# A two-block transformer kernel: the low parts of 18 weight blocks move from VectorE (three: from nowhere) to GpSimd

## The reference, cut to what matters

```
h = rms_norm(x, g_pre) * (1 + scale) + shift          # scale, shift, gate from w_ada
proj = h @ w_in                                        # 2048 x 20032
a  = mla_branch(...) * silu(z_mla);  y_mla = a @ w_mla_proj
bb = dilated_branch(...) * silu(z_dil);  y_dil = bb @ w_dil_proj
x  = x + gate * rms_norm((sigmoid(g1) * y_mla + sigmoid(g2) * y_dil) @ w_o, g_post)
h2 = x @ w_in_a  ->  sparse attention with indexer, gate  ->  @ w_out_a
x  = layer_norm(ALPHA * x + y);  x = x + (p @ w_ple) * sigmoid(x @ w_ple_gate)
x @ w_kv_b, x @ w_q_b  ->  stick-breaking attention, gate  ->  @ w_out_b  ->  norm, gate
```

## Time and profile before

| | |
|---|---|
| median of 3 runs | 2376.17 us (2375.61 to 2376.22) |
| the profiled execution | 2375.65 us, span of its records 2374.3 us |
| TensorE clock granted | full over the whole span |
| TensorE, VectorE, ScalarE, GpSimd busy | 99%, 62%, 48%, 4% |
| split blocks | 781; mean VectorE low part 1.185 us, mean ScalarE high part 1.025 us |
| HBM | 201 GB/s over the span, about 400 in the first 120 us |

### The profile page before, as it was taken

The page is one execution under the profiler, slowest core; times in us unless marked ns, Lnnn a source line. Parts: engine busy times, 40 slices in busy tenths (PEclk is TensorE's granted clock), DMA queues, the critical chain, the costliest instruction groups (busy, mean ns, idle before and its releaser), DMA issues.

```text
span 2374.3 us, 28762 instructions
## 1 busy us (share of the span) xinstructions
PE 2351.3 (99%) x11224; PEld 1965.6 (83%) x11224; DVE 1464.9 (62%) x1997; ACT 1140.7 (48%) x1471; POOL 87.2 (4%) x121
## 2 busy tenths in 40 slices
PE   9999999999999999999999999999999999999999
PEld 5688898988889988888888888888788788888777
DVE  7887765554555455686756675566765555456675
ACT  4344454544445554443444445554545555455453
POOL 0000100000000000000000100000200000000020
PEclk9999999999999999999999999999999999999999
DMA  9986643555554457887655555455665555555565
GB/s 397 401 298 207 196 148 115 173 178 188 188 165 146 139 186 253 288 291 241 213 195 191 181 174 162 163 165 185 223 213 188 169 177 167 185 161 177 187 221 177
DMA packets 131241, 478.98 MB, mean 202 GB/s; under 512 B 15281, under 2 KB 15537, under 8 KB 125985
## 3 DMA queue, kind: packets, MB, share of 16 engines
q1 hardware_dynamic: 126080, 458.41, 58.4%
q0 software_dynamic: 3728, 17.76, 2.1%
q10 hardware_dynamic: 1298, 0.97, 0.1%
HBM read 470.80 MB, written 6.29 MB: 201 GB/s over the span
## 4 chain that ended last, share of the span: by engine, by line
PE 90%; DVE 5%; ACT 2%; DMA 2%; issue 1%; SPq 0%; POOL 0%; ACTq 0%; DVEq 0%; POOLq 0%
PE G L841 25%; PE G L843 25%; PE G L842 25%; PE A L852 4%; DMA ada<-in_weights 2%; DVE wlo L1472 2%; PE A L841 2%; PE A L843 2%; PE A L842 2%; PE A L923 1%; PE A L903 1%; PE G L837 1%; ACT whi L1128 1%; PE A L996 1%; DVE CP L1780 1%
## 5 line engine op out<-in xcount | busy, mean ns | idle before, releaser
L1472 DVE TENSOR_TENSOR wlo<-raw,whi 128x1024 fp32r<-128x1024 f32 (+3 forms) x781 | 922.9, 1185 | 698.2 <-ACT whi L1128 695.9
L1128 ACT ACTIVATE whi<-raw 128x1024 fp32r<-128x1024 f32 (+3 forms) x781 | 800.0, 1025 | 832.3 <-PE G L843 744.5
L841 PE MATMUL G<-whi,XH 128*128 128x512 f32 (+3 forms) x2804 | 1082.1, 386 | 9.1 <-DVE wlo L1472 6.8
L843 PE MATMUL G<-whi,XL 128*128 128x512 f32 (+3 forms) x2804 | 1066.7, 380 | 0.0
L842 PE MATMUL G<-wlo,XH 128*128 128x512 f32 (+3 forms) x2804 | 1065.7, 380 | 0.0
L841 PEld LDWEIGHTS G<-whi,XH 128*128 128x128 f32 x2804 | 526.7, 188 | 105.2 <-DVE wlo L1472 12.7
L843 PEld LDWEIGHTS G<-whi,XL 128*128 128x128 f32 x2804 | 526.3, 188 | 95.1
L842 PEld LDWEIGHTS G<-wlo,XH 128*128 128x128 f32 x2804 | 526.9, 188 | 90.2 <-issue 0.2
L841 PE MATMUL A<-whi,XH 128*128 128x512 f32 x192 | 77.2, 402 | 3.0 <-DVE wlo L1472 3.0
L1486 DVE CUSTOM_DVE_ANT_0 ada<-ada,dil 128x2048 f32<-128x2048 f32 x32 | 75.1, 2347 | 5.0 <-DMA ada<-in_weights 4.9
L842 PE MATMUL A<-wlo,XH 128*128 128x512 f32 x192 | 74.7, 389 | 0.0
(11 more groups left out here) (230 smaller groups left out, 1551.1 us busy)
## 6 DMA issues: line engine op xcount, KB each, us to landing
raw<-in_weights SPq DMA_DIRECT2D x724, 512.0 KB, 3.6
ada<-in_weights SPq DMA_DIRECT2D x32, 1024.0 KB, 11.2
raw<-in_weights SPq DMA_DIRECT2D x80, 384.0 KB, 3.1
raw<-in_weights SPq DMA_DIRECT2D x16, 288.0 KB, 2.9
spill<-nat POOLq DMA_DIRECT2D x8, 512.0 KB, 5.4
CP<-spill POOLq DMA_DIRECT2D x8, 512.0 KB, 6.5
raw<-in_weights SPq DMA_DIRECT2D x8, 336.0 KB, 3.2
FT<-in_xT SPq DMA_DIRECT2D x4, 512.0 KB, 5.7
```

Of the source, the lines that this page charges most:

```text
L841: pe.matmul(acc, xh[:, k, half], wh, start=(k == start), stop=False)
L843: ins = pe.matmul(acc, xl[:, k, half], wh, start=False, stop=(k == end - 1))
L1128: ac.activation(whi[r % NSPL][:, 0:2 * cols], raw[o.home[n]][:, 0:2 * cols], ACT.Copy).then_inc(hi_done, 1)
L1472: ve.tensor_tensor(wlo[r % NSPL][:, 0:2 * cols], raw[o.home[n]][:, 0:2 * cols], whi[r % NSPL][:, 0:2 * cols].bitcast(F32), ALU.subtract).t ...
```

## The change

Slots 18, 21 and 27 leave the set of unsplit slots, so they get a high part and a low part like all others. The low parts of 18 slots (`GP_LOW`), among them these three, are made by GpSimd with the same subtraction, at the take's place in GpSimd's walk. They count on a semaphore of their own, `lo_gp`; `o.low[s]` is the count up to slot s on whichever of the two semaphores slot s uses. TensorE and the loads wait on that one.

```diff
-WHOLE = frozenset([*range(OPENING), 6, 9, 12, 15, 18, 21, 27])
+WHOLE = frozenset([*range(OPENING), 6, 9, 12, 15])
+
+GP_LOW = frozenset([18, 21, 27, 33, 39, 45, 52, 58, 94, 469, 541, 643, 646, 675, 678, 707, 710, 743])
...
+        self.low = {s: sum(x not in self.whole and (x in GP_LOW) == (s in GP_LOW) for x in range(s + 1))
+                    for s in range(len(self.slots))}
@@ TensorE, in slot(s) @@
-                pe.wait_ge(lo_done, o.rank[s] + 1)
+                pe.wait_ge(lo_gp if s in GP_LOW else lo_done, o.low[s])
@@ VectorE, in take(n) @@
+                if o.slot_of[n] in GP_LOW:
+                    return
@@ GpSimd @@
+        def take(n):
+            kind, w, c0, cols, k = plan[n]
+            if kind == "w" and o.slot_of[n] in GP_LOW:
+                r = o.rank[o.slot_of[n]]
+                gp.wait_ge(hi_done, r + 1)
+                gp.tensor_tensor(wlo[r % NSPL][:, 0:2 * cols], raw[o.home[n]][:, 0:2 * cols],
+                                 whi[r % NSPL][:, 0:2 * cols].bitcast(F32), ALU.subtract).then_inc(lo_gp, 1)
...
-                gp.wait_ge(lo_done, o.rank[65] + 1)
+                gp.wait_ge(lo_done, max(o.low[s] for s in range(66) if s not in o.whole and s not in GP_LOW))
...
         for kind, a, b in o.walk:
-            if kind == "move":
+            if kind == "take":
+                take(a)
+            elif kind == "move":
                 move(a)
@@ SyncE, in load(n) @@
-                    sp.wait_ge(lo_done, o.rank[s] + 1)
+                    sp.wait_ge(lo_gp if s in GP_LOW else lo_done, o.low[s])
```

More of the change, by code:

```diff
@@ L642, in first_and_second_block @@
     moved = [sem(f"moved_G{n}") for n in range(4)] + [sem(f"moved_A{n}") for n in range(4)]
-    hi_done, lo_done, modulated, gated = (sem(n) for n in ("hi_done", "lo_done", "modulated", "gated"))
+    hi_done, lo_done, lo_gp, modulated, gated = (sem(n) for n in ("hi_done", "lo_done", "lo_gp", "modulated", "gated"))
     x_hi, x_lo, side_hi, rows_made, rows_gp = (sem(n) for n in ("x_hi", "x_lo", "side_hi", "rows_made", "rows_gp"))
```

## The result

| | before | after |
|---|---|---|
| median | 2376.19 us (2375.61 to 2376.82, 4 runs) | 2387.03 us (2386.08 to 2388.22, 4 runs) |
| the profiled execution | 2375.65 us | 2388.22 us |
| ratio, 95% interval | | 1.0041 (1.0029 to 1.0054) |

The account below looks back on a forecast made before the run. TensorE's matmul issue rate was taken to bound the kernel, except where VectorE hands over a low part late. Terms 0.3 - 1.65 + 0.9 - 1.4 + 1.0 + 6.6 - 0.4 = +5.35 gave 2381.5 us, range 2378 to 2386.

Parts of the forecast that it names:

- opening, to slot 35: Slots 18, 21, 27: 2.2 us of TensorE time saved, lost at slot 33 behind VectorE's product until 120.34; +0.3.
- slot 52: TensorE's idle 1.42 us goes, as GpSimd makes the low part by 172.95; -1.65, between -1.7 and 0.
- slot 94: VectorE's rotation steps and the two adds that empty slot 94's banks slide; +0.9.
- slot 469: VectorE issues first, GpSimd works 1357.6 to 1359.9, and the wait goes; -1.4, or +0.9 if GpSimd is first.
- slot 541: VectorE's later steps and the XL that slot 541 multiplies slide to 1594.0; +1.0.
- three pairs, clock full: Slots 643/646, 675/678, 707/710: two holds per pair delay VectorE's low part between them; +2.2 a pair, +6.6 together.
- slot 743: Idle 0.22 us, one VectorE step behind it, the exponential after that just in time; -0.4, if not +0.6.
- h: Time one 1024-column GpSimd low part keeps VectorE from its own work: 2.15 us, bounds 0 and 2.6.
- A wait costs its idle time and about 0.3: Price of each TensorE wait: its idle time plus about 0.3 us, as the pipe refills.
- Rival 2: No change: the hold does not reach the scans and VectorE's wide product; +0.2, 2376.4 us; chance 0.17.
- Rival 1: Faster: h near 0, every term a gain, 10.1 us with the opening held to 1; 2366 us; chance 0.23.
- rival 3: Slower still: GpSimd first at 469 (+0.9), slots 21 and 33 stall the opening (+1.5); 2385 us; chance 0.07.

Follow-up runs that it names:

- three_gp: The kernel before with only the low parts of slots 52, 469 and 743 on GpSimd; 2372.83 us, ratio 0.9984.
- after_fill4: The changed kernel with four extra 384-column TensorE products, results unused, ahead of slots 645, 677 and 709; 2382.70 us, ratio 1.0024.
- pairs_gp: The kernel before with only the low parts of slots 643, 646, 675, 678, 707 and 710 on GpSimd; 2385.33 us, ratio 1.0036.
- open_dve: The kernel before with slots 18, 21 and 27 split and every low part on VectorE; 2376.74 us, ratio 0.9998.
- open_late: open_dve with ScalarE's wait for a small load moved from slot 22 to slot 42, the loads still issued at 22; 2375.17 us, ratio 0.9995.
- tt_beside: The kernel before plus a 1024-column GpSimd scratch subtraction, which nothing waits for, at the six takes of the pairs; 2386.06 us in one run.
- memset_beside: tt_beside with two GpSimd memsets of scratch tiles in place of each subtraction; 2376.44 us in one run.
- ordered: The kernel before with low parts 52 and 469 on GpSimd and ten VectorE steps issued later, behind the low part due next; 2369.57 us, ratio 0.9967.
- open_gp: The changed kernel with only the low parts of slots 18, 21 and 27 on GpSimd, the other fifteen on VectorE; 2377.58 us, ratio 1.0002.
- best: ordered with slots 18, 21, 27 split on VectorE and ScalarE's small-load step, loads included, moved from slot 22 to 42; 2371.17 us, ratio 0.9976.

## Why the prediction was right in direction and short in size

Each term of the sum, in us longer (+), beside the steps of the table:

| | forecast | after | where else it shows |
|---|---|---|---|
| opening, to slot 35 | +0.3 | +2.7 | +0.1 to +1.8 in kernels whose opening is unchanged |
| slot 52 | -1.65 | -1.67 | three_gp -1.66 |
| slot 94 | +0.9 | +0.87 | after_fill4 +0.87 |
| slot 469 | -1.4 | -1.4 | three_gp -1.37 |
| slot 541 | +1.0 | +1.15 | after_fill4 +1.15 |
| three pairs, clock full | +6.6 | +6.1 | 2.1 each in pairs_gp, after_fill4 |
| clock at half behind two of them | none | +3.4 | gone in after_fill4 |
| slot 743 | -0.4 | -0.2 | three_gp -0.2 |
| clock at half behind slot 745 | none | +1.5 | three_gp, open_dve have it, open_late not |

- **h, the time one GpSimd low part keeps VectorE away: right.** 2.15 was forecast from 128- and 512-column rows. The step of 0.68 takes 2.88 (2.20 more), two scans 3.42 for 1.27 (2.15 more), the wide product up to 4.49 for 2.34 (2.15 more). In the second and third pair the second hold falls on the step behind the scans (L1788, 2.68 for 0.69), at the same price. GpSimd alone takes 2.40 at its shortest, as forecast. That both operands must lie in SBUF shows at slot 45: beside GpSimd's low part VectorE adds a product in PSUM to a tile in SBUF in its usual 0.69 (GpSimd, then VectorE):

```profile
153.66 2.40 POOL L2064 TENSOR_TENSOR wlo<-raw,whi 128x1024 fp32r<-128x1024 f32 x1 [13.34 <-ACT whi L1132]
```
```profile
153.89 0.69 DVE L1556 TENSOR_TENSOR kept<-A,kept 128x512 f32<-128x512 f32 x1 [0.48 <-PE A L847]
```

- **Rival 2 (the hold does not reach scans and the wide product): out.** Both rows just named. tt_beside shows the scans held by work that nothing waits for.
- **Rival 1 (h near 0): out**, by the same rows and by tt_beside against memset_beside. Its gains exist where VectorE has nothing due: three_gp.
- **Slots 52, 94, 469, 541: right to 0.2 us.** At 541 TensorE waits 1.66 us for XL, at 94 1.09 for VectorE's adds, as the prediction named them. At 469 VectorE was first by 0.04 us (1358.39 against 1358.43), so that half of rival 3 did not come true, by little; its other half, a stalled opening, did.

```profile
276.98 0.47 PE L845 MATMUL G<-whi,XH 128*128 128x512 f32 x1 [1.09 <-DVE nat L1565]
...
1594.84 0.47 PE L845 MATMUL G<-whi,XH 128*128 128x512 f32 x1 [1.66 <-DVE XL L2012]
```

- **The pairs: mechanism and size right** (2.0 to 2.1 for 2.2), and they are the loss, by pairs_gp.
- **The step that failed by leaving something out: "A wait costs its idle time and about 0.3".** The forecast itself had waits of 2 to 3 us at slots 645, 677 and 709, where the longest of before for a low part was 1.4 (and 1.79 for XL at slot 745, with the clock full behind it). Behind two of the three the granted clock fell to half for 3.41 us, 1.7 each. after_fill4 keeps the waits, takes the standing still out of them, and the loss goes. The Trainium skill, "TensorE: Matmul & The Clock Gate", section "Part 1: The HAM clock gate (the "warmup" mystery)", says that the clock has two levels and goes by how busy the engine has been of late. The rows show the same two levels, and that rule should have put a price on every wait that the forecast made longer than those in the trace.
- **The opening: mis-sized.** Slot 34 started at 127.64, where 125.0 to 125.7 was forecast. Part of the +2.7 is not the change's: the kernel after is 0.44 late at slot 17 already, ahead of all that was changed, and kernels with the old opening reach slot 35 at +0.07 (ordered), +0.40 (three_gp) and +1.79 (pairs_gp), as their loads land. The three kernels with the whole change reach it at +2.5 to +3.1, from +0.4 to +0.9 at slot 17, so some 2 us are the change's. Of it, slot 23 takes 0.76 (0.3 of that in open_dve too): GpSimd's low part of slot 21 (84.45 to 87.45) holds VectorE, the low part of slot 23 starts at 93.06 and not at 92.12, and TensorE waits 1.01. That is the bound that the forecast named for slot 21. It would have been lost at slot 24 all the same: +1.6 is there at slot 25, from the small load that ScalarE waits for until 95.50; that wait eats what the splits save, as open_late shows, where I had blamed the product of 118.00. In the six kernels with the old opening and that wait in its place it ends 5.3 us behind the load's issue, in those with the three slots split 6.2 to 7.2; why, stays open. open_gp, which runs the same instructions as the kernel after up to there, has it at 94.56, so up to 0.9 is spread between executions. The last +0.8 comes at slot 34, by the hold that the forecast had there, on another instruction. GpSimd, then VectorE, of the kernel after at slots 27 and 33:

```profile
102.23 2.57 POOL L2064 TENSOR_TENSOR wlo<-raw,whi 128x1024 fp32r<-128x1024 f32 x1 [14.78 <-ACT whi L1132]
...
119.90 3.07 POOL L2064 TENSOR_TENSOR wlo<-raw,whi 128x1024 fp32r<-128x1024 f32 x1 [15.10 <-ACT whi L1132]
```
```profile
102.46 4.49 DVE L1492 CUSTOM_DVE_ANT_0 ada<-ada,dil 128x2048 f32<-128x2048 f32 x1
...
120.63 2.35 DVE L1519 SCALAR_TENSOR_TENSOR small<-dil 128x2 f32<-128x2 f32 x1
```

A VectorE instruction on two columns takes 2.35 us behind GpSimd's low part for slot 33. Who holds whom is decided by tenths of a microsecond. At slot 27 of open_gp VectorE is first, by 0.36, keeps its 2.35, and GpSimd takes 4.25; VectorE's next low part then takes 2.23 in its turn:

```profile
101.88 4.25 POOL L2064 TENSOR_TENSOR wlo<-raw,whi 128x1024 fp32r<-128x1024 f32 x1 [14.34 <-ACT whi L1132]
```
```profile
101.52 2.35 DVE L1492 CUSTOM_DVE_ANT_0 ada<-ada,dil 128x2048 f32<-128x2048 f32 x1
```

after_fill4 has the waits of the change and the clock at full speed behind them. Its profiled execution took 2382.89 us against the 2381.0 forecast for one. The 1.9 between them are the opening's 2.2 and the 0.2 each of slots 541 and 743, less the pairs' 0.5; the tenth or two that are left are drift.

## What to carry to other kernels

Moving work to GpSimd beside a VectorE that is not idle moves nothing if both read two operands in SBUF: where GpSimd is first, its instruction comes out of VectorE's time whole, 2.15 us for one that VectorE makes in 1.13. It pays where VectorE's next due time is further off than that (slots 52 and 469), and where VectorE is packed the cure is its order: the low part that is due next goes ahead of the steps that aren't. A wait of TensorE is priced with what its clock does behind it, and an instruction that waits for a small load belongs well behind the load's issue and ahead of nothing that is due.

## What the runs showed of the hardware that I had not expected

- TensorE's granted clock falls to 0.50 for 3.41 us behind waits of 1.8 to 3.2 us, and not each time. In the kernel after it falls behind the waits at 645 (3.00) and 709 (2.84) and not behind that at 677 (2.84); in pairs_gp, with waits of 2.98, 2.83 and 2.83 at the same slots, it falls behind 677 alone; behind the 1.79 at slot 745 it falls in some executions. So the length of the wait alone does not decide it, and which wait is hit can't be forecast from these rows. A fall costs 1.5 to 1.7 us where TensorE would else have run on, and nothing in tt_beside, where it would have waited soon after. It may account for the two groups of times of three_gp, some 1.4 us apart; only the profiled execution of each kernel shows its clock, so this is not shown.
- A scan and VectorE's wide product with its accumulator are held by GpSimd as the two-operand steps are; a memset of GpSimd, 0.95 us for 1024 columns, holds nothing.
- A small load, issued on ScalarE's queue near 88 beside weight loads at 400 GB/s, kept its user waiting until 5.3 us after the issue in the kernel before, 6.4 in open_dve and 7.1 in the kernel after; issued at 143.34 in best, 6.9.
